# One decode step of a hybrid decoder trunk: the whole input projection in three rounded products, weight slots that turn on across layers

## What is computed

```python
def token_mixer(x, pos, past_kv, win_buf, gla_s0, p):
    z = x @ p['w_in']
    q, kv6, nsa_g, gq, gk, gv, g_lr, g_r, mg = jnp.split(z, SPLIT_POINTS, axis=-1)
    ...
    o_nsa = g[..., 0:1] * o_cmp + g[..., 1:2] * o_sel + g[..., 2:3] * o_win
    ...
    o_gla = rms_norm(o_gla, p['gla_norm_g']) * jax.nn.silu(g_r...)
    a = o_nsa @ p['w_nsa_up']
    c = o_gla @ p['w_gla_up']
    y = (jax.nn.sigmoid(m_a) * a + jax.nn.sigmoid(m_c) * c) @ p['w_out']

def trunk_layer(h, ...):
    y, ... = token_mixer(h, ...)
    h = layer_norm(DN_ALPHA * h + y, p['ln1_g'], p['ln1_b'])
    f = jnp.square(jax.nn.relu(h @ p['mlp_w1'])) @ p['mlp_w2']
    return layer_norm(DN_ALPHA * h + f, p['ln2_g'], p['ln2_b'])
```

## Time and profile before

| | us |
|---|---|
| median of 3 runs | 1119.08 (1118.13 to 1120.35) |
| the profiled execution | 1114.8 |
| its span, first to last instruction | 1112.7 |
| mean granted clock of TensorE | 0.943 of full speed |

### The profile page before, as it was taken

How to read it: one execution, slowest core, us unless ns; L and a number is a source line. 1 busy time by engine, 2 the same in 40 slices (tenths; PEclk the granted TensorE clock), 3 DMA queues, 4 the chain that set the end, 5 groups by cost and what they waited for, 6 DMA issues and landing times.

```text
span 1112.7 us, 17708 instructions
## 1 busy us (share of the span) xinstructions
PE 989.2 (89%) x7111; PEld 874.1 (79%) x7111; DVE 633.9 (57%) x1271; ACT 448.6 (40%) x918; POOL 86.8 (8%) x136
## 2 busy tenths in 40 slices
PE   2999898988797999999779899898969889999992
PEld 2976686766696999999669677676758879999991
DVE  4445856556487677534433666654656676764433
ACT  2521224343456656444333012343335565554431
POOL 5001000000103000011300100000010400000111
PEclk9999998999798999999889899899969989999996
DMA  9467651222153465555475684232123525655511
GB/s 247 136 178 198 184 189 38 77 76 76 50 183 114 153 189 189 177 176 179 73 203 166 174 220 166 72 104 76 48 72 117 186 87 181 188 190 179 174 65 39
DMA packets 159218, 155.47 MB, mean 140 GB/s; under 512 B 21282, under 2 KB 154754, under 8 KB 159074
## 3 DMA queue, kind: packets, MB, share of 16 engines
q1 hardware_dynamic: 155634, 142.44, 43.2%
q0 software_dynamic: 3504, 11.91, 3.5%
HBM read 149.27 MB, written 9.24 MB: 142 GB/s over the span
## 4 chain that ended last, share of the span: by engine, by line
PE 71%; DVE 11%; issue 9%; DMA 3%; ACT 2%; SPq 2%; POOL 1%; ACTq 0%; DVEq 0%; POOLq 0%
PE acc L608 14%; PE acc L648 13%; PE acc L649 13%; PE acc L650 13%; PE tr L571 3%; PE sc L764 3%; DMA stw<-in_cache_win_kv 2%; PE sc L811 1%; DVE BIG L1547 1%; DMA wt<-in_w_in 1%; PE o L839 1%; DVE BIG L1494 1%; PE tr L967 1%; PE acc L662 1%; DVE pacc L1538 1%
## 5 line engine op out<-in xcount | busy, mean ns | idle before, releaser
L1464 DVE TENSOR_TENSOR wlo<-wt,whi 128x1024 fp32r<-128x1024 f32 x180 | 218.0, 1249 | 125.4 <-ACT whi L1149 123.7
L648 PE MATMUL acc<-big_parts,whi 128*128 128x264 f32 x896 | 256.4, 286 | 8.5 <-DVE wlo L1464 8.0
L649 PE MATMUL acc<-big_parts,whi 128*128 128x264 f32 x896 | 254.9, 285 | 0.0
L650 PE MATMUL acc<-big_parts,wlo 128*128 128x264 f32 x896 | 254.7, 284 | 0.0
L1149 ACT ACTIVATE whi<-wt 128x1024 fp32r<-128x1024 f32 x180 | 180.5, 1048 | 81.1 <-PE acc L650 68.2
L608 PE MATMUL acc<-hT,wt 128*128 128x264 f32 x768 | 186.7, 399 | 0.0
L648 PEld LDWEIGHTS acc<-big_parts,whi 128*128 128x128 f32 x896 | 169.8, 190 | 10.6 <-issue 9.0
L649 PEld LDWEIGHTS acc<-big_parts,whi 128*128 128x128 f32 x896 | 169.9, 190 | 0.1
L650 PEld LDWEIGHTS acc<-big_parts,wlo 128*128 128x128 f32 x896 | 169.0, 189 | 0.0
L608 PEld LDWEIGHTS acc<-hT,wt 128*128 128x128 f32 x768 | 147.8, 197 | 26.0 <-issue 1.5
L648 PE MATMUL acc<-h_parts,whi 128*128 128x264 f32 x480 | 136.3, 284 | 0.4 <-ACT onT L1138 0.4
(11 more groups left out here) (300 smaller groups left out, 1269.9 us busy)
## 6 DMA issues: line engine op xcount, KB each, us to landing
wt<-in_mlp_w SPq DMA_DIRECT2D x64, 1024.0 KB, 5.2
wt<-in_w_in SPq DMA_DIRECT2D x34, 1024.0 KB, 5.3
BIG<-in_cache_nsa_kv SPq DMA_DIRECT2D x32, 256.0 KB, 3.6
wt<-in_w_out SPq DMA_DIRECT2D x8, 1024.0 KB, 5.3
wt<-in_w_in SPq DMA_DIRECT2D x16, 256.0 KB, 5.1
wt<-in_w_nsa_up SPq DMA_DIRECT2D x16, 256.0 KB, 3.9
wt<-in_w_gla_up SPq DMA_DIRECT2D x8, 512.0 KB, 5.0
out_win_kv_sample<-in_cache_win_kv POOLq DMA_DIRECT2D x2, 2040.0 KB, 13.7
```

What stands on the lines that cost most here:

```text
L648: mm(bank[:, 0:NT], w[0](k0 + k, n), hi(k0 + k), start=(first and k == 0), stop=False)
L649: mm(bank[:, 0:NT], w[0](k0 + k, n), lo(k0 + k), start=False, stop=False)
L650: ins = mm(bank[:, 0:NT], w[1](k0 + k, n), hi(k0 + k), start=False, stop=(last and k == kn - 1))
L1464: V.tensor_tensor(wlo[t % RING][:, 4 * a:4 * a + 4, :], wt[t % RING][:, 1024 * a:1024 * a + 1024].rearrange("p (k n) -> p k n", k=4), whi[ ...
```

## The change

All plain chunks of the input projection become three rounded products. For q0 and q1 the tile is split like the others and the two chunks run as a pair that starts with each piece of x; in layer 0 this tile and the next are rounded and subtracted during the entry norm, in layer 1 at the end of m2. The parts of x get a buffer of their own and are made piece by piece inside the norm. For the 24 other chunks ("gates" e = 0 to 23) a rounding of one chunk's weights (`split_gate_hi`) is put into ScalarE's order and a subtraction (`split_gate_lo`) into VectorE's, two chunks ahead of use; their high parts lie in the buffer of the h parts and, from e = 18 on, in the second `whi`. Slots now turn on across the layers (`slot_of`), so that a layer's first loads wait only for the tile four before. To make room, four buffers share memory (keys and transposed probabilities, sample probabilities and states, window pages and probabilities), the sample values move from the fourth to the third attention pass, and the descriptor space of GpSimd's DMAs is halved.

```diff
+    def slot_of(l, t):
+        return (l * TILES + t) % RING
+    def hi_buf(t):
+        return (t + 1) % 2 if t < SPLIT_A else (t - SPLIT_B) % 2
...
+        x_parts = sb("x_parts", [128, 2, KD, NT], F32R)
+        x_hi, x_lo = x_parts[:, 0], x_parts[:, 1]
...
                 def load(t, parts):
-                    free, v = slot_free(t)
-                    sp.wait_ge(free, v)
+                    if l * TILES + t >= RING:
+                        free, v = tile_used(*divmod(l * TILES + t - RING, TILES))
+                        sp.wait_ge(free, v)
...
# TensorE
+                def gate_chunk(e):
+                    name, n = gate_name(e), e % 2
+                    hi, lo = gate_hi(e), wlo[slot_of(l, gate_tile(e))]
+                    wait(gate_lo_d.sem, gate_lo_d.at(l, e + 1))
+                    split_chunk(name, ...)
+                split_pair(["q0", "q1"], split_in(T_Q), lambda k: x_hi[:, k, :], lambda k: x_lo[:, k, :],
+                           lambda k: wait(x_lo_d.sem, x_lo_d.at(l, k + 1)))
...
-                    chunk(f"gla{4 + s}" if s < 4 else f"gr{s - 4}", w, s % 2, hk)
+                    gate_chunk(s)
...
                     elif k == 2:
                         gla_scores(0)
+                        sample_values()
                     elif k == 3:
-                        sample_values()
+                        sample_rows_tr()
...
# ScalarE
+            split_hi(0, T_Q)
             act.wait_ge(ini["sum"], 1)
...
+            split_hi(0, T_Q + 1)
...
                 A_(hT[:, c, :], hT[:, c, :], ACT.Identity, bias=lv[:, 8 + c:9 + c]).then_inc(h_ready.sem, 1)
+                x_part_hi(0, c)
...
-                split_hi(1)
-                split_hi(2)
+                split_hi(l, T_Q + 2)
                 chunks = [q0 ... gla3]
                 for i, (name, dst) in enumerate(chunks):
                     evac(name, dst)
...
+                split_gate_hi(0)
+                split_gate_hi(1)
...
                 for s in range(NS):
                     ...
+                    if s + 2 < NS:
+                        split_gate_hi(s + 2)
+                split_gate_hi(8)
...
                     if 2 * k + 2 < 16:
                         gate_sigmoid(2 * k + 2)
                     ...
+                    if 2 * k + 12 < GATES:
+                        split_gate_hi(2 * k + 12)
                     if 2 * k + 3 < 16:
                         gate_sigmoid(2 * k + 3)
+                    if 2 * k + 13 < GATES:
+                        split_gate_hi(2 * k + 13)
...
                     if t < 14:
                         split_hi(l, T_M2 + t + 2)
+                    elif l + 1 < LAYERS:
+                        split_hi(l + 1, t - 14)
# VectorE
+                split_gate_lo(0)
+                split_gate_lo(1)
                 for s in range(NS):
                     b = tr_in(f"pairs{s}")
                     ...
                     V.tensor_copy(kTs[:, s % 2, :, 0:PAST], ...).then_inc(tb.done, 1)
+                    if s + 2 < NS:
+                        split_gate_lo(s + 2)
                     if s >= 5:
                         pe_product((s - 5) // 2, (s - 5) % 2)
...
+                split_gate_lo(10)
...
                     if k < 8:
                         unit_prob(2 * k)
                         unit_prob(2 * k + 1)
+                    if 1 <= k and 2 * k + 11 < GATES:
+                        split_gate_lo(2 * k + 11)
                     ...
+                    if 2 * k + 12 < GATES:
+                        split_gate_lo(2 * k + 12)
...
-    nc = bacc.Bacc("TRN2", target_bir_lowering=False, num_devices=1)
+    nc = bacc.Bacc("TRN2", target_bir_lowering=False, num_devices=1, dynamic_dma_scratch_size=8192)
```

More of the change, by code:

```diff
@@ L756, in _ @@
                 for j, name in enumerate(("hidk", "hidv")):
-                    s, per, v = landed(T_CMP + j)
-                    wait(s, l * per + v)
+                    wait(*landed(l, T_CMP + j))
                     b = take(sc, name)
-                    w = wt[(T_CMP + j) % RING]
+                    w = wt[slot_of(l, T_CMP + j)]
                     for lp in range(16):
@@ L1111, in _, with split_hi, x_part_hi @@
             act.sem_inc(ob.done, 2)
+            def split_hi(l, t, halves=(0, 1)):
+                if 0 in halves:
+                    if t in (T_Q, T_Q + 1) and l > 0:
+                        act.wait_ge(*tile_used(l - 1, TILES - 2 + t))
+                    elif t == SPLIT_B + 1:
+                        act.wait_ge(acc.ready, acc.filled(l, "mg15"))
+                    elif T_Q + 2 <= t < SPLIT_A or t > SPLIT_B + 1:
+                        act.wait_ge(*tile_used(l, t - 2))
+                    act.wait_ge(*landed(l, t))
+                for a in halves:
+                    A_(whi[hi_buf(t)][:, 4 * a:4 * a + 4, :],
+                       wt[slot_of(l, t)][:, 1024 * a:1024 * a + 1024].rearrange("p (k n) -> p k n", k=4), ACT.Copy).then_inc(w_hi.sem, 1)
+            def x_part_hi(l, c):
+                act.wait_ge(h_ready.sem, h_ready.at(l, c + 1))
+                A_(x_hi[:, c, :], hT[:, c, :], ACT.Copy).then_inc(x_hi_d.sem, 1)
+            split_hi(0, T_Q)
             act.wait_ge(ini["sum"], 1)
@@ L1529, in pe_product @@
                     if half == 0:
-                        slot, per, v = landed(T_CMP + j)
-                        dve.wait_ge(slot, l * per + v)
-                    w = wt[(T_CMP + j) % RING]
+                        dve.wait_ge(*landed(l, T_CMP + j))
+                    w = wt[slot_of(l, T_CMP + j)]
                     for lp in range(8 * half, 8 * half + 8):
```

197 lines of the change are left out of this document (104 added, 93 removed), and 2 rows, old and new, of the table t_plan.

## The result

The changed kernel took 1121.6 us (median of 20 runs, 1118.6 to 1125.6) against 1119.0 for the kernel before (20 runs): a ratio of 1.0037 [1.0022, 1.0052]. It is 0.4% slower, where 0.9% faster was predicted. The profiled execution took 1120.2 us, its span 1118.1.

A forecast was written before the change was run, and what follows sets the result against it. TensorE, 89% busy, was taken to set the pace. Start -1.8, turn +6.7, cache loop -7.5, compression +2.9 and passes +10.0 made 10.3 us gained: 1119.1 to 1108.8, rounded to 1109; range 1095 to 1126 for 8 in 10.

The forecast's parts named there:

- the cache loop: Eight shorter chunks, with added subtractions in VectorE's queue: 4.7 us lost in layer 0, 2.8 in layer 1, 7.5 together.
- passes and compression: Fourteen attention-pass chunks gain 5.0 us a layer, 10.0 in all; two chunks behind the compression gain 2.9 in all.
- the start: Start of layer 0: query products begin 0.3 us late and half clock costs 1.5, so 1.8 us lost.
- VectorE's order: In the cache loop, subtractions wait for ScalarE's rounding between key copies and pair copies; a pass saves 0.4 us, not 0.72.
- lower bound for the loop: In the cache loop, 13 us lost: all ten subtractions on the path, nothing saved, 12.2 a layer, less 5.8.
- The turn from layer 0 to 1: Earlier tile loads shorten last m2 evacuation to third query chunk from 25.3 to 19.3 us; 6.7 us gained with clock.
- The kv rounding: At the start and the turn, 2.0 us on ScalarE ahead of the evacuations of q0 and q1, so TensorE waits.
- The low part ahead of the maximum: Before the attention passes, the first subtraction stands ahead of the cache maximum: 1.2 us lost in full, each layer.
- the two chunks behind the compression: They shrink by 1.4 us a layer and the hidden part still hides: 2.9 us gained in all.
- The second rival: In the attention passes, low parts come onto the softmax chain: 15 us lost instead of 10 gained; middle 1126; chance 0.19.
- Edits at nothing: Moved gated-product wait, shared buffers and halved descriptor space for GpSimd's loads were all priced at no cost or gain.
- The rivals: TensorE's saving nearly whole, half case 1095 (0.17); passes slowed, 1126 (0.19); no gain at the turn, 1116 to 1118 (0.12).

The follow-up runs named there:

- Ring4: The changed kernel with four buffers for cache pages in place of two; 1111.8 us, ratio 0.9949 to the kernel before.
- hi3: The changed kernel with a third rounded-weights buffer in the loop, rounding the chunk after next ahead of the present evacuation; 1113.1 us, ratio 0.9972 to the kernel before.
- ev_first: The changed kernel with ScalarE evacuating q0 and q1 ahead of the rounding of the first kv tile; 1112.7 us, ratio 0.9947 to the kernel before.

## Why the prediction was wrong

**The step that failed is the cache loop.** It was priced at 7.5 us lost (4.7 and 2.8) and lost 21.2 by the trace and 19.4 by the times. The forecast's sum was 10.3 gained; with the loop's measured size in its place it turns to 2 to 3 lost, and 2.6 was found. That this fits so closely is in part luck: passes and compression gained 5.4 less than forecast by the trace and the start lost 1.1 more, while the end of the program gave 2.7 that the forecast put at nothing. Three things were wrong in that step. It took the pages as given: they do not occur in it, though the earlier trace rows had shown a wait for loads elsewhere, and the loop's own chain was not read. Ring4 shows the pages' part as 7.4 and 5.4 us. It was right on the pace of the first two passes (10.3 us; 5.4 and 5.0 measured) and on a step of 8 with the position products, but had nothing like the 12.2 to the fifth sample, for a page. And it let the longer gaps cost 0.6 us of clock, while the stretch ran at 0.87. What it said of VectorE's order was right (waiting for roundings between pair copies; steps of about 8 with the position products): hi3 shows it as 4.8 and 3.7 us. Even its lower bound for the loop, 13 lost in both layers, was too small, since it had only subtractions in it and no load. It is also not what its words say: with ten subtractions on the path and nothing saved it would be 24.4, from which the saving of 5.8 a layer was taken off all the same.

**The turn from layer 0 to 1 was right.** From the last m2 evacuation to the third query chunk the forecast said 19.3 us. ScalarE's and TensorE's timelines, beside the earlier trace rows:

```profile
555.47 0.39 ACT L1172 ACTIVATE onT<-acc 128x264 f32<-128x264 f32 x1 [2.51 <-PE acc L659]
...
572.60 2.00 ACT L1135 ACTIVATE whi<-wt 128x1024 fp32r<-128x1024 f32 x2 [2.43 <-PE acc L673]
574.51 0.65 ACT L1172 ACTIVATE BIG<-acc 128x264 f32<-128x264 f32 x2
579.75 0.39 ACT L1172 ACTIVATE BIG<-acc 128x264 f32<-128x264 f32 x1 [4.58 <-PE acc L659]
```

```profile
575.02 0.36 PE L657 MATMUL acc<-x_parts,whi 128*128 128x264 f32 x1 [2.46 <-DVE wlo L1480]
```

575.02 - 555.47 = 19.55, and to the end of that chunk 6.4 us were gained against 6.7. The kv rounding (572.60) still blocks the two evacuations, as said; ev_first is its price.

**The start** lost 2.9 us in the profiled execution and 1.3 to 3.0 in others, against 1.8. The mechanism is the one described: a pause, here of 2.46 us, and half clock after it (records of 0.42 us where those at full clock take 0.28):

```profile
38.86 0.36 PE L657 MATMUL acc<-x_parts,whi 128*128 128x264 f32 x1 [2.46 <-DVE wlo L1480]
...
40.09 0.42 PE L657 MATMUL acc<-x_parts,whi 128*128 128x264 f32 x1
```

**Passes and compression** were forecast at 12.9 us gained (10.0 and 2.9); the times give 11.5, the two profiled executions 7.5. The low part ahead of the maximum cost 1.1 and 1.45 us, as priced (1.2). Of the two chunks behind the compression, layer 0 got 1.3 of 1.4 us; in layer 1 0.8 was lost instead, as the hidden products began at half clock behind the gaps at the loop's end (the first 32 took 9.66 us instead of 7.55). From the first score product to the first up chunk 4.8 us a layer came out of the 6.2 forecast. The second rival, that low parts come onto the softmax chain and the passes lose, was not seen.

**Edits at nothing.** The halved descriptor space was not nothing but a gain of 2.7 us at the end of the program by the traces (2.2 by the times on one chip, with an interval that reaches none, and 8.7 in the runs before). The shared buffers showed no cost that could be told from the spread.

The rivals missed the outcome too: the slower side was given to the attention passes (0.19), not to the loop. The range held 1121.6, but for a reason that stood in no case; that is luck.

## What to carry to other kernels

Before an instruction of a busy engine is shortened, read the chain of waits inside that very stretch: an engine can be 91% busy and still not set the pace alone, when a chain of loads and copies stands level with it. Work that is added to a queue in front of a copy that frees a load buffer is paid at the next load, late and with the clock lost in the pause; give the loads more buffers, put big loads behind small urgent ones, and let roundings run ahead of evacuations. Mended so, the kernel was 2.9 to 3.2% faster than before instead of 0.4% slower.

## What was not expected of the hardware

Halving the space for GpSimd's DMA descriptors shortened the time between the last output's issue and the end of the span from 9.8 to 7.1 or 7.2 us, in all 18 profiled executions with it, while the last output landed 4.1 us after its issue in the changed kernel as before. What the rest of that time is, no trace shows. Two pauses of TensorE of 2.46 us (ended at 38.86 and 575.02) were each followed by a stretch at half clock (records of 0.42 us from 40.09 and from 575.83 on; the granted clock was 0.50 from 40 to 42 and from 577 to 579 us). And the same page load, behind the same 1 MB in the same queue, took 4.75 us to land in one execution and 7.4 in another; in the kernel before with the halved space it took 7.1 in layer 1. What makes the difference, no run here shows.
